# Three changes inside an mLSTM cell: split operands for one product, turned sample numerators, and a denominator moved into the variance

## What is computed

```python
qk = jnp.einsum('bthd,bshd->bhts', qc, kc) * w
num = s_inter[..., None] * jnp.einsum('bthd,bhde->bhte', qc, cm) + jnp.einsum('bhts,bshe->bhte', qk, vc)
den = s_inter * jnp.einsum('bthd,bhd->bht', qc, nv) + jnp.sum(qk, axis=-1)
h = num / jnp.maximum(jnp.abs(den), jnp.exp(-m_t))[..., None]
...
kw = kc * w_s.transpose(0, 2, 1)[..., None]
c_new = dec[..., None, None] * cm + jnp.einsum('bshd,bshe->bhde', kw, vc)
...
y = head_layernorm(o * h, gn) + skip.astype(f32) * xc.astype(f32)
```

## Time and profile before

| what | value |
| --- | --- |
| median of 3 runs | 2201.51 us (2201.0 to 2205.11) |
| profiled execution | 2201.16 us |
| its span in the trace | 2199.4 us |
| mean granted TensorE clock | 0.998 |
| PE busy | 2156.8 us, 98% of the span |
| DVE busy | 1244.7 us, 57% |
| POOL busy | 1203.1 us, 55% |
| ACT busy | 423.2 us, 19% |
| cell of the mLSTM, from the value transposes of its first head on | about 1317 to 1602 us |

### The profile page before, as it was taken

The page is one execution under the profiler, slowest core; times in us unless marked ns, Lnnn a source line. Parts: engine busy times, 40 slices in busy tenths (PEclk is TensorE's granted clock), DMA queues, the critical chain, the costliest instruction groups (busy, mean ns, idle before and its releaser), DMA issues. The chain is left out here.

```text
span 2199.4 us, 38981 instructions
## 1 busy us (share of the span) xinstructions
PE 2156.8 (98%) x15839; PEld 2019.4 (92%) x15839; DVE 1244.7 (57%) x2095; ACT 423.2 (19%) x780; POOL 1203.1 (55%) x1228
## 2 busy tenths in 40 slices
PE   9989899999999999999999999999999999999998
PEld 9988789989999999999999995587699999999997
DVE  6888875454625344676557645772754364435263
ACT  6224541222000000121202113421422220000002
POOL 7675666526656655666657650032254365665663
PEclk9999999999999999999999999999999999999999
DMA  6224344212222222224433323552332122222221
GB/s 219 77 87 145 112 144 192 78 39 78 77 95 78 77 82 89 76 92 153 152 145 136 142 100 141 203 192 78 120 137 75 39 79 95 77 79 94 77 78 62
DMA packets 41809, 235.95 MB, mean 107 GB/s; under 512 B 4672, under 2 KB 10048, under 8 KB 16584
## 3 DMA queue, kind: packets, MB, share of 16 engines
q1 hardware_dynamic: 24512, 157.57, 20.2%
q10 hardware_dynamic: 17160, 76.38, 9.1%
HBM read 200.05 MB, written 33.89 MB: 106 GB/s over the span
## 5 line engine op out<-in xcount | busy, mean ns | idle before, releaser
L501 POOL TENSOR_TENSOR wlo<-raw,whi 128x512 fp32r<-128x512 f32 (+1 forms) x684 | 827.4, 1219 | 112.6 <-ACT whi L1253 69.9
L494 POOL TENSOR_SCALAR whi<-raw 128x512 fp32r<-128x512 f32 x512 | 365.3, 714 | 824.1 <-PE psum L596 771.3
L596 PE MATMUL psum<-xnh,whi 128*128 128x288 f32 (+1 forms) x2784 | 607.6, 296 | 13.2 <-DVEq L210 3.6
L596 PE MATMUL psum<-xnh,wlo 128*128 128x288 f32 (+1 forms) x2784 | 603.9, 295 | 0.0
L596 PE MATMUL psum<-xnl,whi 128*128 128x288 f32 (+1 forms) x2784 | 603.8, 295 | 0.0
L596 PEld LDWEIGHTS psum<-xnh,whi 128*128 128x128 f32 x2784 | 451.9, 189 | 20.4 <-issue 11.8
L596 PEld LDWEIGHTS psum<-xnh,wlo 128*128 128x128 f32 x2784 | 451.8, 189 | 0.0
L596 PEld LDWEIGHTS psum<-xnl,whi 128*128 128x128 f32 x2784 | 451.8, 189 | 0.0
L596 PE MATMUL psum<-hh,whi 128*128 128x288 f32 x992 | 212.0, 295 | 2.1 <-DVE hl L2330 2.1
L596 PE MATMUL psum<-hl,whi 128*128 128x288 f32 x992 | 211.8, 294 | 0.0
L596 PE MATMUL psum<-hh,wlo 128*128 128x288 f32 x992 | 210.7, 293 | 0.0
(11 more groups left out here) (459 smaller groups left out, 2766.1 us busy)
## 6 DMA issues: line engine op xcount, KB each, us to landing
raw<-in_w SPq DMA_DIRECT2D x145, 1024.0 KB, 4.8
C<-in_C ACTq DMA_DIRECT2D x4, 1024.0 KB, 4.8
o_cp<-mvt ACTq DMA_DIRECT2D x4, 1024.0 KB, 3.9
o_cs<-C ACTq DMA_DIRECT2D x4, 1024.0 KB, 6.5
t_xc<-xc ACTq DMA_DIRECT2D x3, 1152.0 KB, 7.3
t_z<-mv ACTq DMA_DIRECT2D x3, 1152.0 KB, 4.1
t_q<-mq ACTq DMA_DIRECT2D x3, 1152.0 KB, 4.2
t_k<-mk ACTq DMA_DIRECT2D x3, 1152.0 KB, 4.2
```

Of the source, the lines that this page charges most:

```text
L494: pool.tensor_scalar(whi[:, s, c], raw[:, s, c], 1.0, 1.0, ALU.mult, ALU.mult).then_inc(S("slab_hi"), 1)
L501: ins = pool.tensor_tensor(wlo[:, s, c], raw[:, s, c], whi[:, s, c].bitcast(F32), ALU.subtract)
L596: ins = pe.matmul(bank(g, 2 * m + b)[:, 0:t1 - t0], W[wi][:, kk, m0 + m, :], r[:, kk, t0:t1], start=(at_first and wi == 0 and r is rh), st ...
```

## The change

The change has five parts.
1. For n = 0, 1 and 3 (`CELL_SPLIT`), POOL splits `mvt` into `xnh`/`xnl` tiles 0 to 3 and `mkt` into `mkh` and `mkl` (`cell_split`, 16 instructions a head), and PE does `kv` as 48 fp32r matmuls in place of 16 fp32 ones. `kv` now runs with the token block outermost. `mkh` lies where `mv` lies, so the load of the next `mv` moves behind `kv`.
2. The samples' numerators are made with features on the partitions at once: 16 products of `C0` by `qs` and 4 of `vt5` by `wts`, 64 columns each, at the end of `den`. The copy to `tm` and the four transposes go.
3. ACT's order for a head becomes: copies to `mkt`, two `high_y`, absolute denominators, two `high_y`, the sums, the loads.
4. The product with 1/den is left out, since a layer norm of num/den equals (num - mean)/sqrt(var(num) + EPS den^2). DVE makes `rs` = EPS x 4 x den^2 instead, and adds it to the first square.
5. The semaphore `x_again` is replaced by one that exists already.

The diff without its context lines, cut to what matters:

```diff
+CELL_SPLIT = (4, 4, 0, 4)
+CELL_SPLIT_BY = [sum(CELL_SPLIT[:n]) for n in range(ML_H + 1)]
...
+        mvs = ExitStack()
+        mkh = sb("mkt_high", [P, ML_T, T], F32R, on=mvs)
+        mvs.close()
...
+        mks = ExitStack()
+        mkl = sb("mkt_low", [P, NTB, ML_DH], F32R, on=mks)
+        mks.close()
...
+        def mv_split(j):
+            return xnh[:, j, 0:ML_DH], xnl[:, j, 0:ML_DH]
...
-            third = SL["ml_out", 0, 2]
-            with pool.Fori(mem0 // 2 + len(MEM_SLABS) // 2 + 1, third // 2) as i:
+            def cell_split(n):
...
+                m, at = CELL_SPLIT[n], 4 * CELL_SPLIT_BY[n]
+                pool.wait_ge(S("cell_vt"), n + 1)
+                for j in range(m):
+                    pool.tensor_scalar(mv_split(j)[0], mvt[:, j, :], 1.0, 1.0, ALU.mult, ALU.mult).then_inc(S("cell_split"), 1)
+                for j in range(m):
+                    pool.wait_ge(S("cell_split"), at + m + j)
+                    hi, lo = mv_split(j)
+                    pool.tensor_tensor(lo, mvt[:, j, :], hi.bitcast(F32), ALU.subtract).then_inc(S("cell_split"), 1)
+                at += 2 * m
+                pool.wait_ge(S("cell_kt"), n + 1)
+                for j0 in range(0, m, 2):
+                    for j in (j0, j0 + 1):
+                        pool.tensor_scalar(mkh[:, j, 0:ML_DH], mkt[:, j, :], 1.0, 1.0, ALU.mult, ALU.mult).then_inc(S("cell_split"), 1)
+                    for j in (j0, j0 + 1):
+                        pool.wait_ge(S("cell_split"), at + 2 * j0 + 2 + (j - j0))
+                        pool.tensor_tensor(mkl[:, j, :], mkt[:, j, :], mkh[:, j, 0:ML_DH].bitcast(F32), ALU.subtract).then_inc(S("cell_split"), 1)
...
+            third, first = SL["ml_out", 0, 2], SL["ml_out", 1, 0]
+            with pool.Fori(mem0 // 2 + len(MEM_SLABS) // 2 + 1, first // 2) as i:
...
+            for n in range(first // 2 * 2, third // 2 * 2):
+                split(n % 2, n // 2)
+                if n == first:
+                    cell_split(0)
+                    cell_split(1)
+                if n == SL["ml_out", 0, 0]:
+                    cell_split(3)
...
-                pe.wait_ge(S("cell_qs"), n + 1)
-                pe.wait_ge(S("cell_smp"), n + 1)
-                pe.wait_ge(S("cell_c"), 16 * (n + 1))
-                for d in range(ML_T):
-                    mm(B[2][0:TS, :], qs[:, d, :], C0[:, d, :], d == 0, False)
-                mm(B[2][0:TS, :], wts[:], vt5[:], False, True).then_inc(S("bank_filled"), 1)
...
+                pe.wait_ge(S("cell_qs"), n + 1)
...
+                pe.wait_ge(S("cell_smp"), n + 1)
...
-                pe.wait_ge(S("bank_read"), n + 1)
+                pe.wait_ge(S("cell_c"), 16 * (n + 1))
...
-                    ins = pe.transpose(B[3][:, TS * e:TS * e + TS], tm[0:TS, 1, P * e:P * e + P], ident[0:TS, 0:TS])
+                    out = B[3][:, TS * e:TS * e + TS]
+                    for d in range(ML_T):
+                        mm(out, C0[:, d, P * e:P * e + P], qs[:, d, :], d == 0, False)
+                    ins = mm(out, vt5[:, P * e:P * e + P], wts[:], False, True)
...
-                for d in range(ML_T):
-                    for j in range(NTB):
-                        ins = mm(B[d], mkt[:, j, P * d:P * d + P], mvt[:, j, :], j == 0, j == NTB - 1)
-                        if n + 1 == ML_H and (d, j) == (0, 0):
-                            ins.then_inc(S("slab_begun"), 1)
+                m, at = CELL_SPLIT[n], 4 * CELL_SPLIT_BY[n] + 2 * CELL_SPLIT[n]
+                for j in range(NTB):
+                    if j < m:
+                        pe.wait_ge(S("cell_split"), at + 2 * (j - j % 2) + 3 + j % 2)
+                    for d in range(ML_T):
+                        c = slice(P * d, P * d + P)
+                        if j < m:
+                            hi, lo = mv_split(j)
+                            ins = mm(B[d], mkh[:, j, c], hi, j == 0, False)
+                            if n + 1 == ML_H and (d, j) == (0, 0):
+                                ins.then_inc(S("slab_begun"), 1)
+                            mm(B[d], mkl[:, j, c], hi, False, False)
+                            ins = mm(B[d], mkh[:, j, c], lo, False, j == NTB - 1)
+                        else:
+                            ins = mm(B[d], mkt[:, j, c], mvt[:, j, :], j == 0, j == NTB - 1)
...
-                act.wait_ge(S("bank_filled"), ML_H + 1)
+                act.wait_ge(S("bank_filled"), 1)
...
-                    ch.mark(act.activation(rs[:, t0:t1], bank(g, 2 + b)[:, 0:HALF], ACT.Ln, bias=epst[:]))
+                    ch.mark(act.activation(rs[:, t0:t1], bank(g, 2 + b)[:, 0:HALF], ACT.Ln, bias=0.0))
...
-                    high_y(n - 1, 0)
-                    high_y(n - 1, 1)
...
-                act.wait_ge(S("bank_filled"), n + 1)
-                act.activation(tm[0:TS, 1, 0:ML_DH], bank(GR["cell", h, "den"], 2)[0:TS, :], ACT.Copy).then_inc(S("bank_read"), 1)
+                if n:
+                    high_y(n - 1, 0)
+                    high_y(n - 1, 1)
+                g = GR["cell", h, "den"]
+                group_ready(act, g)
+                act.activation(tm[:, 1, 0:TP], bank(g, 0), ACT.Abs)
+                act.activation(tm[:, 1, TP:T], bank(g, 1)[:, 0:TS], ACT.Abs)
+                ch.mark(act.activation(qs[:].rearrange("p e t -> p (e t)"), bank(g, 3)[:, 0:ML_T * TS], ACT.Copy),
+                        free[g % 2], S("cell_abs"))
...
-                    load(mv[:], A["t_v"][nxt], "cell_v")
-                g = GR["cell", h, "den"]
-                group_ready(act, g)
-                act.activation(tm[:, 1, 0:TP], bank(g, 0), ACT.Abs)
-                act.activation(tm[:, 1, TP:T], bank(g, 1)[:, 0:TS], ACT.Abs)
-                ch.mark(act.activation(qs[:].rearrange("p e t -> p (e t)"), bank(g, 3)[:, 0:ML_T * TS], ACT.Copy),
-                        free[g % 2], S("cell_abs"))
...
+                if nxt is not None:
+                    load(mv[:], A["t_v"][nxt], "cell_v")
...
-                step(lambda: tt(tm[:, 1, :], tm[:, 1, :], en, ALU.max))
-                step(lambda: v.reciprocal(tm[:, 1, :], tm[:, 1, :]))
+                step(lambda: stt(tm[:, 1, :], en, 1e18, tm[:, 1, :], ALU.min, ALU.max))
+                step(lambda: stt(rs[:], tm[:, 1, :], EPS * ML_DH / P, tm[:, 1, :], MUL, MUL))
...
-                step(lambda: tt(sz[:], sz[:], tm[:, 1, :].unsqueeze(1).to_broadcast([P, ML_T, T]), MUL))
...
-                        ins = v.tensor_copy(ss[:], tm[:, 0, :])
+                        ins = stt(ss[:], rs[:], 1e-36, tm[:, 0, :], ADD, ADD)
```

More of the change, by code:

```diff
@@ L1161, in _ @@
             out_slab(0, 1, order=(4, 5, 6, 7), stop=False, close=False, first=False, columns=(0,))
-            pe.wait_ge(S("bank_read"), ML_H + 1)
+            pe.wait_ge(S("bank_read"), 1)
             out_slab(0, 1, order=(4, 5, 6, 7), stop=False, close=False, first=False, columns=(1,))
@@ L1183, in _, with rstd @@
             act.activation(rsc[:, 0:1], epst[:], ACT.Copy)
-            def rstd(g, out, width=T):
+            def rstd(g, out, width=T, eps=epst[:]):
                 group_ready(act, g)
                 for b, (t0, t1) in enumerate(((0, HALF), (HALF, T)) if width == T else ((0, width),)):
-                    ins = act.activation(out[:, t0:t1], bank(g, b)[:, 0:t1 - t0], ACT.Ln, bias=epst[:])
+                    ins = act.activation(out[:, t0:t1], bank(g, b)[:, 0:t1 - t0], ACT.Ln, bias=eps)
                     ch.mark(ins)
@@ L1436, in _ @@
             act.wait_ge(S("fin_copied"), RET_H)
-            load(x, A["xT"][:, :, 0:T], "x_again")
+            load(x, A["xT"][:, :, 0:T], "x_loaded0")
             for a in range(2):
@@ L1709, in _ @@
                 if nxt is not None:
-                    rstd(GR["cell", h, "var"], rs)
+                    rstd(GR["cell", h, "var"], rs, eps=0.0)
                 else:
@@ L2205, in _ @@
             v.sem_inc(S("arena_free"), 1)
-            v.wait_ge(S("x_again"), 16)
+            v.wait_ge(S("x_loaded0"), X_LOADED[0] + 16)
             residual_and_norm([GR["rs_out", i] for i in range(4)], 1, "cross0")
```

## The result

| | before | changed |
| --- | --- | --- |
| median | 2202.65 us (20 runs) | 2210.14 us (2202.06 to 2217.23, 20 runs) |
| ratio to before, over the paired runs on record (the medians alone give 1.0034) | 1 | 1.0030, 95% interval 1.0020 to 1.0039 |
| profiled execution, its span | 2201.16, 2199.4 us | 2202.06, 2200.0 us |
| mean granted TensorE clock | 0.998 | 0.993 profiled, 0.987 to 0.995 over the runs |
| DVE, POOL busy | 1244.7, 1203.1 us | 1239.3, 1257.8 us |

The forecast was 2193.6 us, within 2189.3 to 2198.0. The changed kernel is slower by 0.3%: the prediction was wrong in size and in sign. The profiled execution is the fastest of the 20, so its trace understates the loss.

What follows compares the result with a forecast made beforehand. PE was taken to bound the kernel, with DVE having least room. Gains of 11.25 us less 0.4, 0.8, 2.3 and 0.2 left 7.55 us off 2201.16: 2193.6 us, range 2189.3 to 2198.0.

Steps and rivals of the forecast that it cites:

- the den term: Denominators and sample numerators: 0.1 us lost to 0.3 won a head; 0.15 taken, 0.6 us over four heads.
- DVE's delay: DVE beside POOL's splits: 7.0 us later in n = 1 and in n = 3, range 5 to 9.
- 3.1 us late in n = 3: DVE's room before the `C0` update in n = 3: -3.1 us, of which 2.3 us taken as loss in the chain.
- The wait for `C0`: Head n = 0: PE's wait for the load of `C0` goes, a gain of 1.42 us.
- The 0.33 us before `kv`: Head n = 1: PE's wait for a bank ACT frees goes, a gain of 0.33 us.
- the slower `cell_out`: Sign: DVE's `cell_out` lines in n = 1 and 3 between 1.0 and 1.7 us, not all 0.82 and 0.76.
- PE's wait for DVE behind n = 1: Sign: PE waits on DVE before the scores following n = 1; 0.8 us lost.
- the longer stretch from the last `kvs` to the output projection: Sign at the end of the last head: this stretch longer by some 2 us.
- two signs of being wrong: The prediction is wrong if PE waits before `kv`, or if `cell_out` keeps its pace.
- the engines exclude each other fully: Rival: DVE and POOL never overlap, DVE 4.9 us later in each of two heads; 2203.4 us, chance 0.09.
- POOL is late: Rival: POOL's splits late, PE waits at `kv`, ending 9.6 us late in two heads; 2209.6 us, chance 0.05.
- Slower: Outcome of the whole kernel being slower than before; chance 0.05, against 0.80 for faster and 0.15 for same.

Runs made afterwards that it cites:

- e4: The changed kernel with the 16 `C0` by `qs` products a head 128 columns wide, second half never read; 2204.03 us, ratio to before 1.0000.
- e2: The kernel before with only the turned sample numerators and the changed order inside `den`; 2221.05 us, ratio to before 1.0072.
- e1: The changed kernel with plain sample numerators again (64 x 512 product, ACT's copy, four transposes), first in the group; 2202.05 us, ratio to before 0.9991.
- e9: The kernel of e4 with the split in n = 0 and n = 1 only; 2199.10 us, ratio to before 0.9981.
- e7: The kernel of e6 with the split in two heads only, n = 3 being fp32 again; 2200.72 us, ratio to before 0.9982.
- e6: The kernel of e1 with the `ones` products placed ahead of the plain numerators; 2205.04 us, ratio to before 1.0011.
- e12: The kernel of e7 with n = 0 alone split; 2200.48 us, ratio to before 0.9981.
- e3: The changed kernel with each narrow numerator tile ahead of one quarter of `num` in n = 0, 1 and 3; 2208.83 us, ratio to before 1.0025.
- e10: The kernel of e7 with splits of 4, 2, 0, 2 token blocks by head; 2196.32 us, ratio to before 0.9962.
- e5: The changed kernel without its split, every head's `kv` fp32 again; 2220.76 us, ratio to before 1.0075.
- e8: The kernel of e1 with the reciprocal and the product with `sz` back on DVE; 2219.84 us, ratio to before 1.0069.
- e11: The kernel of e7 with no split in any head; 2201.97 us, ratio to before 0.9987.

## Why the prediction was wrong

**The step that failed** is the den term: "Taking the tail off gives about 4.6. So this is between 0.1 us lost and 0.3 us won a head." Two things were wrong in it. The size: a tile takes 1.40 us, four of them 5.61, so the part loses 0.7 us a head and gains nothing. The upper bound of 0.125 us a record was none: eight records on full weights took 1.04 us from start to start, and the two on 64 rows behind them 0.36, 0.18 each. With the seam before the first tile the group `den` is 0.8 us longer in each head, 3.8 us off the forecast over four. And the method: the products were priced by their own duration alone, at the clock of the row they came from. What a stretch of 40 narrow records does to the clock of what follows was in no term, no rival and no bound. It is 1.63 us in `num` for n = 0 and 1, 1.45 in the projection behind the tiles of n = 2, and 4.7 in n = 3 (2.55 in the tiles, 2.14 in `num`): 9.4 us in the profiled run. e4 against the changed kernel shows 0.30%, some 6.6 us. That is a net figure: by the profiles e4 pays 0.8 us for its wider tiles and 3.45 for the wait and the fall at the end of n = 3, which the changed kernel doesn't. e2, which has this part alone, is 0.72% slower than before.

**DVE's delay was sized right, and its price was put in the wrong place.** 7.0 us were forecast for n = 1 and for n = 3, and `cell_out` grew by 7.67 and 6.75. The changed kernel doesn't show its cost, since PE's own lateness covers it (idle 1.14 us before the `C` update in n = 1, 1.34 in n = 3). With the clock kept, it comes out: 3.1 us late in n = 3 were forecast, and PE waits 2.17 us in e1 and 1.45 in e4. But it comes before `kvs`, not behind the update; a PE that waits there loses the clock as well, which about doubles it; and in n = 1 the delay surfaces in a place that the forecast didn't look at, the load of `mk`. Of the loads in ACT's queue the prediction said only that `mv` starts later. The split of n = 3 costs more than it gains (e9 against e4, e7 against e6), and in e6's order that of n = 1 gives nearly all of its gain back (e12 against e7).

**What held.** `kv` took 11.28 us for n = 0 (1352.27 to 1363.55) and 11.26 for n = 1, with a step of 0.23 us a matmul, for 10.9 forecast; 2.6 us won a head instead of 3.0, 1.2 us less in all. n = 2 kept 13.9. POOL's 12 instructions beside DVE ended at 1402.4, and PE never waited for them; 17.8 us from 1384.61, where 18.0 was forecast. The wait for `C0` went, but 0.90 us of it came back as a wait for DVE ahead of the first `ones` product (1332.83). The 0.33 us before `kv` went. The wait before the key transposes shrank from 0.72 to 0.24 us in n = 1, but the value transposes start 0.29 us later there; net this gives 0.6 us over the heads, which had not been counted. Of the signs that the prediction named, no wait at `kv`, no wait on `C0` and the slower `cell_out` came true. PE's wait for DVE behind n = 1 did not, nor the longer stretch from the last `kvs` to the output projection (26.25 us, 26.14 before). Neither of its two signs of being wrong came, and it was wrong all the same.

**The rivals.** That the engines exclude each other fully was out: a low part and a DVE instruction share 1.6 us, where 2.1 was the rival's sum. "POOL is late" was the case for slower, and named the wrong engine. Slower had 0.05, and it had it because every mechanism considered was a wait or the pace of the instruction itself.

**The sum now.** It closes for the cell in the two profiled runs, where the four stretches make 281.81 us before and 284.95 changed: 3.1 us longer, where 7.55 shorter was forecast. The 10.7 us between are the clock 9.4, the group `den` 3.8, `kv` 1.2 and the wait ahead of `ones` 0.9, less 3.6 for DVE's delay (3.7 forecast in all its terms, 0.1 shown), 0.6 for the transposes and 0.4 because `kv` starts earlier behind `num` than forecast. For the median it is an estimate: 2202.65 and 3.1 make 2205.8 us. Over the 20 runs a mean granted clock lower by 0.001 goes with some 1.7 us more (a straight line through their times and clocks), and the profiled run had 0.993 where their median is 0.991; that is another 3.4 us. The last microsecond to 2210.14 stays open.

## What to carry to other kernels

A rewrite that turns a few wide matmuls into many narrow ones has two prices: its own duration, and the clock of the wide products behind it. PE's busy share shows neither, so read the granted clock in windows of 2 us across the seam; padding to twice the columns was nearly free (0.05 us in 1.40) and kept the clock (e4), and so did spreading the narrow products between wide ones (e3). When GpSimd takes work for TensorE beside a busy VectorE, give it only as much as VectorE's slack holds in each stage (here half splits in two heads in place of whole ones: 0.5% between e6 and e10, and 0.25% over no split, where whole splits in two heads added nothing measurable). When you move work on one engine, follow what a third engine does between two others: ACT's one copy behind `C0` by `qs` held up DVE by up to 4.5 us a head in e6 and the kernels built on it. And look for the loads whose buffers VectorE frees, not for its own next result alone.

## What had not been expected of the hardware

- Granted clock 0.50 with TensorE busy 2.00 of 2.00 us, behind 64-column fp32 products (n = 0, 1 and 3 of the changed kernel, and n = 0 of e2 and e5 with an idle GpSimd; 0.57 in n = 2). With 128 columns, 1.00; with the same 64-column products spread between quarters of `num` (e3), 1.00.
- A wait of TensorE of 1.45 (e4), 2.17, 3.43 (e3), 3.80, 4.03 and 6.56 us ahead of `kvs`, each with the lower clock during or behind it; after a wait of 2.03 us ahead of the scores (e7) they took their usual 8.87 us. So the length of a wait alone doesn't tell; what stands around it wasn't varied.
- Eight records of 128 x 64 took 1.00 or 1.10 us and eight of 128 x 128 took 1.16: between 64 and 128 columns the width hardly sets the pace.
- Falls of the clock outside the changed code, at 130 to 170 us in e2, e3, e4, e6, e8, e9, e11 and e12 and at 1320 to 1340 us in e2, e3, e5, e7, e8, e10 and e11. They add some 1 to 4 us to single profiles and their cause is open; for that reason the text goes by the ratios, and the stretches only say where.
